# Storing four of nine output blocks inside the last projection of a two-layer decoder

## The reference

```
x = x + mix @ w_out
x = x + jax.nn.sigmoid(x @ w_pg) * (p_i @ w_pp)
...
y = (x * rsqrt(mean(x * x) + EPS)) * g_final
```

## Time and profile before

| | |
|---|---|
| three runs | 1164.29, 1162.62, 1164.19 us; median 1164.19 |
| profiled execution | 1162.91 us, span 1161.0 |
| TensorE matmul, weight loads | 98%, 97% of the span |
| VectorE, ScalarE, GpSimd | 58%, 42%, 41% |
| granted TensorE clock | 1.000 |
| last of 40 slices of the span: DMA | 150 GB/s |

### The profile page before, as it was taken

The page is one execution under the profiler, slowest core; times in us unless marked ns, Lnnn a source line. Parts: engine busy times, 40 slices in busy tenths (PEclk is TensorE's granted clock), DMA queues, the critical chain, the costliest instruction groups (busy, mean ns, idle before and its releaser), DMA issues.

```text
span 1161.0 us, 18804 instructions
## 1 busy us (share of the span) xinstructions
PE 1138.4 (98%) x7288; PEld 1122.2 (97%) x7288; DVE 678.6 (58%) x1262; ACT 488.4 (42%) x1097; POOL 481.1 (41%) x655
## 2 busy tenths in 40 slices
PE   5999999999999999999999999999999999999997
PEld 5999999999999999999999999999999999999997
DVE  2453868787854444466634476878785544444444
ACT  5311556666553222333321146575755322233334
POOL 3634445656562323222434434465656423222220
PEclk9999999999999999999999999999999999999999
DMA  8632110111122211111063211111111211211103
GB/s 211 183 91 56 38 52 21 37 38 37 38 55 62 63 49 46 56 49 50 21 183 89 78 38 37 38 37 38 37 38 37 62 55 57 64 46 46 46 2 150
DMA packets 127953, 70.44 MB, mean 61 GB/s; under 512 B 43157, under 2 KB 123861, under 8 KB 127833
## 3 DMA queue, kind: packets, MB, share of 16 engines
q1 hardware_dynamic: 122400, 61.33, 18.6%
q10 hardware_dynamic: 5464, 7.92, 2.8%
HBM read 59.10 MB, written 6.76 MB: 57 GB/s over the span
## 4 chain that ended last, share of the span: by engine, by line
PE 83%; DVE 8%; ACT 5%; issue 2%; DMA 1%; POOL 1%; ACTq 0%; DVEq 0%
PE ring L442 76%; PE aux L480 1%; PE aux L456 1%; DVE yc L1238 1%; DMA xnat<-in_x_prompt_dram 1%; DVE st L1111 1%; ACT comb L794 1%; ACT ptcp L794 1%; PE aux L465 1%; DVE qst L1139 1%; DVE st L1115 1%; DVE kst L1142 1%; DVE ptcp L1109 1%; ACT ptcp L867 1%; DVE yc L1236 1%
## 5 line engine op out<-in xcount | busy, mean ns | idle before, releaser
L442 PE MATMUL ring<-act,ws 128*128 128x352 f32 x6048 | 993.6, 322 | 0.6 <-DVE kT L1183 0.3
L442 PEld LDWEIGHTS ring<-act,ws 128*128 128x128 f32 x6048 | 965.1, 188 | 2.7 <-DVE act L1013 0.5
L425 POOL TENSOR_TENSOR ws<-stage,ws 128x256 fp32r<-128x256 f32 x352 | 277.6, 820 | 535.2 <-ACT ws L726 535.2
L735 ACT ACTIVATE act<-tmp 128x352 fp32r<-128x352 f32 x120 | 59.7, 497 | 233.8 <-DVE tmp L1274 143.7
L419 POOL TENSOR_TENSOR stage<-stage,gT 128x256 f32<-128x256 f32 x208 | 133.6, 672 | 23.0 <-DMA stage<-in_w_in_dram 12.2
L726 ACT ACTIVATE ws<-stage 128x1024 fp32r<-128x1024 f32 (+1 forms) x84 | 91.5, 1090 | 94.1 <-PE ring L442 78.1
L1006 DVE TENSOR_TENSOR act<-tmp,act 128x352 fp32r<-128x352 f32 x120 | 70.4, 586 | 52.9 <-ACT act L735 52.1
L1300 DVE TENSOR_TENSOR tmp<-ring,gate 128x352 f32<-128x352 f32 x48 | 25.2, 524 | 83.5 <-ACT gate L942 83.5
L398 POOL TENSOR_SCALAR_AFFINE_SELECT pw<-pw 128x512 fp32r<-128x512 f32 x56 | 37.3, 669 | 79.7 <-ACT pw L872 75.3
L1272 DVE TENSOR_TENSOR tmp<-ring,act 128x352 f32<-128x352 f32 x48 | 25.2, 525 | 66.9 <-PE ring L442 66.9
L442 PE MATMUL ring<-pT,ws 128*128 128x352 f32 x288 | 53.7, 322 | 0.0
(11 more groups left out here) (191 smaller groups left out, 998.0 us busy)
## 6 DMA issues: line engine op xcount, KB each, us to landing
stage<-in_w_in_dram SPq DMA_DIRECT2D x36, 512.0 KB, 3.8
stage<-in_w_in_dram SPq DMA_DIRECT2D x32, 256.0 KB, 3.8
stage<-in_w_pg_dram SPq DMA_DIRECT2D x16, 512.0 KB, 3.7
rot<-raw ACTq DMA_DIRECT2D x32, 132.0 KB, 2.4
stage<-in_w_out_dram SPq DMA_DIRECT2D x32, 128.0 KB, 2.9
stage<-in_w_out_dram SPq DMA_DIRECT2D x16, 256.0 KB, 3.1
out_dram<-xnat SPq DMA_DIRECT2D x6, 512.0 KB, 3.2
xnat<-in_x_prompt_dram SPq DMA_DIRECT2D x4, 512.0 KB, 7.7
```

The lines of the kernel that those rows point to most:

```text
L425: rest = nc.gpsimd.tensor_tensor(ws[:, s, 1, k:k + 2, :], stage[:, s, k:k + 2, :], ws[:, s, 0, k:k + 2, :].bitcast(F32), ALU.subtract)
L442: mm = nc.tensor.matmul(out, ws[:, w % 2, wp, kw, :], x[:, xp, kx, cs], start=(i == 0 and wp == 0 and xp == 0), stop=(i == n - 1 and wp == 1))
L735: nc.scalar.activation(dst, tmp[:, s % 2, :], ACT.Copy).then_inc(S["hi_out"], 1)
```

## The change

In the last layer the last six slots are reordered: (6,0), (6,1), (7,0), (7,1), (6,2), (7,2). After four of them the first two thirds of all features are done, and with them blocks 0 to 4. The norm has two parts, blocks 0 to 4 and 5 to 8. The sums of the first part come after slot 22, which is now (6,2). In slot 23 TensorE turns blocks 0 and 1 between the p-matmuls and the other 24, block 2 ahead of the fourth feature tile (after nine of the 24 matmuls) and block 3 ahead of the fifth (after twelve); block 4 comes after the slot, then the sums of the second part and blocks 5 to 8. The means and the root of the first part move into slot 22 of VectorE and ScalarE. VectorE scales block 0 there, and block 2 in slot 23 ahead of its multiply; ScalarE evicts blocks 1 and 3 ahead of the last Sigmoid. A Sqrt on one column of ones, whose result is not used, follows that Sigmoid. `ynat` holds blocks 0 to 4 instead of 0 and 1; `xnat`, which lies over activations that the last slot reads, holds the others. `Y_AT` is changed to fit.

```diff
@@ -162,7 +162,7 @@
...
                 xfin, _ = place("xfin", [P, KT, T], F32, off)
-                ynat, _ = place("ynat", [P, 2, D], F32, lo)
+                ynat, _ = place("ynat", [P, 5, D], F32, lo)
@@ -230,10 +230,21 @@
...
         y_turns.append(aux[:, 2:4, :].rearrange("p a n -> p (a n)"))
-        PARTS = ((0, 2), (2, 5), (5, NB + 1))
+        PARTS = ((0, 5), (5, NB + 1))
...
         Y_OF = ((0, 2, 5, 7), (1, 3, 4, 6, 8))
-        Y_AT = (0, 3, 0, 1, 2, 0, 1, 2, 0)
+        Y_AT = (0, 3, 0, 3, 1, 2, 0, 1, 3)
+        Y_INSIDE = {3: 2, 4: 3}
+        LAST = [(6, 0), (6, 1), (7, 0), (7, 1), (6, 2), (7, 2)]
+        def c_order(l):
+            order = [(s // NCH, s % NCH) for s in range(B_SLOTS)]
+            return order if l < DEPTH - 1 else order[:-len(LAST)] + LAST
+        def y_slots(part):
+            return B_SLOTS - len(LAST) + LAST.index((KT - 1, part + 1)) + 1
@@ -241,7 +252,7 @@
...
-            return ynat[:, b, :] if b < 2 else xnat[:, b, :]
+            return ynat[:, b, :] if b < PARTS[0][1] else xnat[:, b, :]
@@ -429,13 +440,15 @@
...
         def _(pe):
-            def group(g, w, x, tiles, cs, waits=None, last=None):
+            def group(g, w, x, tiles, cs, waits=None, inside=None):
...
                 for i, (kw, kx) in enumerate(tiles):
+                    if inside and i in inside:
+                        inside[i]()
@@ -541,8 +554,8 @@
...
-                norm_sums((DEPTH - 1) * NSQ + (KT - 2) * NCH, part)
-                pe.wait_ge(S["sq_out"], DEPTH * B_SLOTS - 2 + part)
+                norm_sums((DEPTH - 1) * NSQ + (KT - 3) * NCH + part + 2, part)
+                pe.wait_ge(S["sq_out"], (DEPTH - 1) * B_SLOTS + y_slots(part))
@@ -552,7 +565,7 @@
...
                 t0 = b * P if b < NB else LASTB
-                pe.wait_ge(S["y_scaled"], B_SLOTS - 2 + y_part(b))
+                pe.wait_ge(S["y_scaled"], y_slots(y_part(b)))
@@ -679,34 +692,34 @@
...
                 g0 += B_SLOTS
-                for f in range(KT):
+                for s, (f, c) in enumerate(c_order(l)):
...
                     pe.wait_ge(w_lo, w + 1)
-                    for c in range(NCH):
-                        s = NCH * f + c
-                        if s == 0:
-                            pe.wait_ge(S["p_hi"], 3 * (l + 1))
-                            pe.wait_ge(S["p_lo"], 3 * (l + 1))
-                        group(g0 + 2 * s, w, pT, [(KT + k, k) for k in range(KP)], cols(c))
-                        waits = None
-                        if f == 0:
-                            waits = lambda i, c=c: (S["mid_split"], l * B_SLOTS + NCH * i + c + 1)
-                        group(g0 + 2 * s + 1, w, xa, [(k, k) for k in range(KT)], cols(c), waits)
-                        if l == DEPTH - 1 and s == B_SLOTS - 2:
-                            last_sums(0)
-                            turn_y(0)
-                            pe.wait_ge(S["mean_done"], DEPTH + 1)
-                            turn_y(1)
-            pe.wait_ge(*y_stored(1))
+                    if s == 0:
+                        pe.wait_ge(S["p_hi"], 3 * (l + 1))
+                        pe.wait_ge(S["p_lo"], 3 * (l + 1))
+                    group(g0 + 2 * s, w, pT, [(KT + k, k) for k in range(KP)], cols(c))
+                    waits = None
+                    if f == 0:
+                        waits = lambda i, c=c: (S["mid_split"], l * B_SLOTS + NCH * i + c + 1)
+                    inside = None
+                    if l == DEPTH - 1 and s == B_SLOTS - 1:
+                        turn_y(0)
+                        pe.wait_ge(S["mean_done"], DEPTH + 1)
+                        turn_y(1)
+                        inside = {i: (lambda b=b: turn_y(b)) for i, b in Y_INSIDE.items()}
+                    group(g0 + 2 * s + 1, w, xa, [(k, k) for k in range(KT)], cols(c), waits, inside)
+                    if l == DEPTH - 1 and s == B_SLOTS - 2:
+                        last_sums(0)
+            turn_y(4)
+            pe.wait_ge(*y_stored(3))
             last_sums(1)
-            turn_y(2)
-            turn_y(3)
-            turn_y(4)
+            turn_y(5)
+            turn_y(6)
+            turn_y(7)
             pe.wait_ge(S["mean_done"], DEPTH + 2)
-            last_sums(2)
-            for b in range(5, NB + 1):
-                turn_y(b)
+            turn_y(8)
@@ -926,22 +939,23 @@
...
                 g0 += B_SLOTS
-                for s in range(B_SLOTS):
-                    f, c = s // NCH, s % NCH
+                for s, (f, c) in enumerate(c_order(l)):
...
                     if l == DEPTH - 1 and s == B_SLOTS - 1:
-                        y_root(0)
                         y_evict(1)
+                        y_evict(3)
...
                     nc.scalar.activation(gate[:, s % 2, :], src, ACT.Sigmoid).then_inc(free[g % 4], 1)
+                    if l == DEPTH - 1 and s == B_SLOTS - 2:
+                        y_root(0)
                     if l == DEPTH - 1 and s == B_SLOTS - 1:
-                        y_root(1)
+                        nc.scalar.activation(nr[:, 6, 0:1], ones[:, 0:1], ACT.Sqrt)
@@ -949,8 +963,8 @@
...
                         last = xfin[:, f, cols(c)]
-                    if s >= 2 * NCH:
-                        sc.wait_ge(S["acc_done"], l * NSQ + s - 2 * NCH + 1)
+                    if f >= 2:
+                        sc.wait_ge(S["acc_done"], l * NSQ + NCH * (f - 2) + c + 1)
@@ -958,9 +972,9 @@
...
                         nc.scalar.activation(last, last, ACT.Copy, scale=gT[:, DEPTH, f:f + 1]).then_inc(S["y_scaled"], 1)
-            y_evict(3)
-            y_root(2)
-            for b in (4, 6, 8):
+            y_evict(4)
+            y_root(1)
+            for b in (6, 8):
@@ -1015,14 +1029,14 @@
...
-                f, c = s // NCH, s % NCH
+                f, c = c_order(l)[s]
...
                 if f >= 2:
-                    ve.wait_ge(S["acc_done"], l * NSQ + s - 2 * NCH + 1)
+                    ve.wait_ge(S["acc_done"], l * NSQ + NCH * (f - 2) + c + 1)
@@ -1293,8 +1305,7 @@
...
                     if l == DEPTH - 1 and s == B_SLOTS - 1:
-                        y_norm(0)
-                        scale_y(0)
+                        scale_y(2)
@@ -1304,13 +1315,14 @@
...
                         V.tensor_tensor(x, x, t, ALU.add).then_inc(S["out_split"], 1)
+                        if s == B_SLOTS - 2:
+                            y_norm(0)
+                            scale_y(0)
...
             y_norm(1)
-            scale_y(2)
-            y_norm(2)
...
```

## The result

Over 20 runs each, the change has a median of 1166.43 us and the kernel before 1164.23; the ratio is 1.0019 (95% interval 1.0013 to 1.0026). The profiled execution took 1165.19 us with a span of 1163.3, which is 2.3 more than before. Of these, the forecast had 0.2.

The account below looks back on a forecast made before the run. TensorE bounds the kernel to 1137.7, then a tail ending in a full-rate store stream. That stream is 1.30 shorter but starts 1.48 later: span 1161.2, +0.2, median 1164.4 us, range 1162.4 to 1166.8.

Parts of the forecast that it names:

- rival B: TensorE at its lower clock from the five blocks' sums on: some 8 us, half of it median 1168; chance 0.06.
- The forecast's own range: Median 1163.3 to 1165.6, from the bounds of a turn, ScalarE's 0.38 and the scatter of the runs.
- signs of being wrong: Bytes ending before 1159 or after 1162, hole after block 5, inner turns over 1.1, clock under 1.00 before 1156, slot-20 wait.
- Weights, order, turns inside the group, covers: Slot 20's weights 1.37 early, reordering free, inner turns 0.91 each, covers 0.7 and 1.5 for turns 2 and 3.
- TensorE to the last matmul: Last slot's matmuls end at 1147.91 against 1145.86: +2.05, bounds +1.9 to +2.5; five blocks' sums 2.13.
- ScalarE: Around the last Sigmoid: 0.38 lost to its table load, Sigmoid at 1148.65, Sigmoid to Square 1.88 against 2.06.
- rival C: ScalarE needs time behind table loads: 0.96 at both in the path, span 1163.1, median 1166.3; chance 0.03.
- The last blocks: Behind the last slot: TensorE waits 1.3 for the Square, block 5 scaled at 1154.90, block 8 out at 1156.83.
- The stores: Last stream starts with block 5: 1154.90 + 0.83, 4.45 of bytes to 1160.18, then 1.0 to span 1161.2.
- The change at full clock: Whole kernel without a clock fall: span 1161.2, +0.2; 1164.4 on the median.
- Against: Reason against lower clock in the last slot: today 3.73 us without ring matmuls, 1.11 idle, are followed by 0.159 a matmul.

Follow-up runs that it names:

- e1: Changed kernel plus eight extra 352-column matmuls in TensorE's wait between the halves of the last four sums; ratio to the kernel before 1.0010.
- e6: Changed kernel with 128-column sums at the layer boundary and in the last layer; ratio to the kernel before 1.0003, tail 28.80.
- c1: Kernel before, no edit, profiled again; span 1162.5, mean clock 0.997, tail 28.40, clock fall at the layer boundary.
- e4: Kernel before plus six extra one-column matmuls behind the first part's four; ratio to the kernel before 1.0007, tail 30.22.
- c2: Kernel before with the 18 one-column sums at the layer boundary made 128 columns wide; ratio to the kernel before 0.9999.
- e2: Changed kernel with the five blocks' sums spread inside slot 22's matmuls instead of behind them; ratio to the kernel before 1.0009.
- e3: Changed kernel with sums inside slot 22 and eight extra matmuls in TensorE's wait; ratio to the kernel before 1.0004, tail 29.22.
- v1: Changed kernel, sums inside slot 22, turns 0 to 2 spread over the last slot, 3 and 4 behind it, VectorE scaling block 3; ratio to before 0.9990.
- e5: Changed kernel with last-layer norm sums of 128 columns instead of one, boundary sums left at one; ratio to the kernel before 1.0003.
- v2: As v1, but the sums of blocks 0 to 4 stay behind slot 22 in one stretch; ratio to the kernel before 0.9999, tail 28.81.

## Why the prediction held, and which step failed

The range held the time and the verdict "within 0.2%" came out, at its edge. That was luck, as 2.0 of the 2.2 us are not the forecast's. In the tail of the profile 1.8 to 1.9 are rival B's, which had 0.06 (30.58 for the change, 28.68 and 28.80 without falls in e1 and e6). The forecast's own range, 1163.3 to 1165.6, was missed, and three of its signs of being wrong came out: a granted clock under 1.00 before 1156 (from 1141.2), a hole after block 5 (1160.3), and bytes that end after 1162 (1162.4).

- **Weights, order, turns inside the group, covers.** As forecast: no wait at slot 20 (it begins at 1123.18 without idle time), 0.92 and 0.93 for the inner turns, no wait before them.
- **TensorE to the last matmul.** The sums took 2.28 for 2.13. The matmuls end at 1149.67, that is 1.66 later than the 1147.91 forecast once 0.10 of a later start is taken off; 1.23 for the turns of blocks 0 and 1 and 0.35 for nine matmuls, 1.58 together, are the lower clock.
- **ScalarE.** 0.51 lost to the table for 0.38; Sigmoid to Square 1.88 for 1.88. The trace after has 0.01 and 0.02 behind its loads, so rival C is not seen here. Nor is the drain that the Trainium skill, "ScalarE: Activation LUTs", section "What ACT_TABLE_LOAD costs", puts beside each load.
- **The last blocks.** TensorE's wait is 1.39 for 1.3. Block 5 is ready at 1156.77 for 1154.90.
- **The stores.** The reckoning of the end stands: 1156.77 + 0.83 + 4.45 + 1.0 = 1163.05. The second stretch makes block 7 late and adds the last 0.25 by the hole at 1160.3. So the first stretch costs some 1.6 us at the end, the second little, because the stream hides it.
- **The change at full clock.** Forecast +0.2; e1's tail is +0.30 and e6's +0.42.

The step that failed is B's "Against: today 3.73 us without matmuls of the ring, 1.11 of them idle, are followed by 0.159 a matmul". It let today's place, with 8 one-column instructions, a turn and a wait, stand for 20 one-column instructions in a row, and one execution stand for all. The clock did not fall there in the second profile of the kernel before either (c1), but it did with 12 more one-column instructions in that place (e4). The place that B named was right (behind the five blocks' sums), its price too high: some 1.6 us at the last matmul and 1.8 to 1.9 at the end, not 4. That such sums can be followed by a fall could have been read at the layer boundary, where they stand too; but there the first profile happened to have no fall, so only the runs' scatter pointed to it.

## What to carry to other kernels

A granted clock of 1.00 in one profile says that the clock did not fall in that execution. Where TensorE does a run of one-column matmuls, price the work behind it at both levels, look at several executions, and spread the sums among wide matmuls or make them wide. Wide sums cost 0.08 us in e6, but whether the kernel gets faster has to be measured: c2 lost its falls and was no faster. Spread sums brought back a wait of 0.46 in e2 and e3, until v1 moved the turns too. When a stream of stores ends last, removing blocks from it gains only what the first remaining block does not lose.

## What the runs showed of the hardware that was not expected

The clock fell without idle time ahead of it: from 1137.49 to 1141 the records of the weight loads stand without a gap, and the windows there go from 1.00 to 0.54. The Trainium skill, "TensorE: Matmul & The Clock Gate", section "Part 1: The HAM clock gate", gives the clock two levels and puts the lower one behind idleness, and says that the moment of the change to the higher one varies between executions. The two levels agree (0.50 and 1.00). What varies here is more than a moment: whether the clock falls at all (the same boundary sums with 7.67 and 9.19 behind them). "Idle", as time without instructions, does not cover this case: the engine was busy on every instruction, with one column each in the sums. With 128 columns in the same instructions the falls went (in the last layer alone 15 of 20 runs at 0.996 or less against none of 11 in e5; with the boundary 1 run of 20 at 0.999 or more against 10 of 11 in e6). In v2 and at the boundary the fall came without a turn ahead of it. Whether turns alone, without sums ahead of them, would let it fall was not tried.
